# Expert weights in units of one expert's half matrix (16 KB a partition) instead of a quarter of both experts (2 x 8 KB)

## The reference

```python
def expert_block(args):
    tok, e = args
    xb = x_pad[tok]
    gate = jnp.minimum(xb @ w_gate[e] + b_gate[e], SWIGLU_LIMIT)
    up = jnp.clip(xb @ w_up[e] + b_up[e], -SWIGLU_LIMIT, SWIGLU_LIMIT)
    h = gate * jax.nn.sigmoid(SWIGLU_ALPHA * gate) * (up + 1.0)
    return h @ w_down[e] + b_down[e]
```

## Time and profile before

| what | us |
|---|---|
| time, median of 3 runs | 3278.82 (3273.98 to 3283.41) |
| the profiled execution | 3282.47 |
| its span on the core | 3280.6 |
| TensorE busy (matmuls) | 3042.0 |
| vector engine busy | 957.1 |
| scalar engine busy | 476.9 |
| experts: 16 pairs, start of the first gate to the end | 2239.3 to 3280.6 |
| one pair in the middle | 63.60 |

### The profile page before, as it was taken

The page is one execution under the profiler, slowest core; times in us unless marked ns, Lnnn a source line. Parts: engine busy times, 40 slices in busy tenths (PEclk is TensorE's granted clock), DMA queues, the critical chain, the costliest instruction groups (busy, mean ns, idle before and its releaser), DMA issues.

```text
span 3280.6 us, 48447 instructions
## 1 busy us (share of the span) xinstructions
PE 3042.0 (93%) x19571; PEld 2258.1 (69%) x19571; DVE 957.1 (29%) x2650; ACT 476.9 (15%) x628; POOL 102.6 (3%) x194
## 2 busy tenths in 40 slices
PE   8999999999999896886969999958999999999995
PEld 7888888888888785776868888835455445445542
DVE  2342442442343064745630000031112111111214
ACT  2122122122121202011100000000111101111111
POOL 2100100100100000000000000000000000000000
PEclk9999999999999897988989999958999999999998
DMA  6234223224245341422324446526999999999994
GB/s 188 84 98 129 89 94 129 92 91 129 96 100 157 113 129 49 132 73 83 112 75 151 151 153 230 205 65 242 409 408 404 397 408 408 394 409 407 398 404 191
DMA packets 326069, 662.19 MB, mean 202 GB/s; under 512 B 41856, under 2 KB 271360, under 8 KB 275456
## 3 DMA queue, kind: packets, MB, share of 16 engines
q1 hardware_dynamic: 325920, 659.85, 54.7%
HBM read 657.73 MB, written 2.10 MB: 201 GB/s over the span
## 4 chain that ended last, share of the span: by engine, by line
PE 64%; issue 16%; DVE 9%; DVEq 4%; ACT 2%; ACTq 1%; POOL 1%; POOLq 1%; SPq 1%; DMA 0%
PE bank L950 13%; PE bank L831 10%; PE bank L595 9%; PE bank L939 7%; PE bank L981 7%; PE bank L852 3%; PE bank L997 3%; DVE arena L1519 2%; DVE arena L1521 2%; DVEq L1518 2%; PE bank L811 2%; PE bank L655 1%; PE bank L664 1%; PE bank L778 1%; PE bank L668 1%
## 5 line engine op out<-in xcount | busy, mean ns | idle before, releaser
L595 PE MATMUL bank<-arena 128*128 128x256 f32 x4096 | 937.1, 384 | 0.0
L595 PEld LDWEIGHTS bank<-arena 128*128 128x128 f32 x4096 | 770.0, 191 | 114.0 <-issue 7.7
L950 PE MATMUL bank<-arena 128*64 128x512 f32 x2048 | 442.2, 592 | 0.7 <-ACT arena L1219 0.7
L950 PEld LDWEIGHTS bank<-arena 128*64 128x64 f32 x2048 | 146.9, 137 | 292.8 <-issue 291.1
L831 PE MATMUL bank<-arena 128*128 128x256 f32 x1536 | 333.3, 380 | 7.4 <-ACTq L1174 7.4
L831 PEld LDWEIGHTS bank<-arena 128*128 128x128 f32 x1536 | 292.9, 191 | 47.8 <-issue 7.7
L939 PEld LDWEIGHTS bank<-arena 128*128 128x128 f32 x1024 | 224.7, 311 | 15.4 <-issue 12.2
L981 PE MATMUL bank<-arena 128*64 128x512 f32 x1024 | 224.9, 597 | 7.7 <-ACT arena L1229 7.7
L939 PE MATMUL bank<-arena 128*128 128x128 f32 x1024 | 227.8, 384 | 3.1 <-DVEq L1718 3.1
L796 PE MATMUL bank<-arena 128*128 128x256 f32 x1024 | 222.3, 379 | 0.0
L796 PEld LDWEIGHTS bank<-arena 128*128 128x128 f32 x1024 | 194.6, 190 | 26.5
(11 more groups left out here) (289 smaller groups left out, 2318.2 us busy)
## 6 DMA issues: line engine op xcount, KB each, us to landing
arena<-in_w_in_dram SPq DMA_DIRECT2D x72, 2048.0 KB, 8.7
arena<-in_w_gate_dram SPq DMA_DIRECT2D x64, 2048.0 KB, 16.9
arena<-in_w_up_dram SPq DMA_DIRECT2D x64, 2048.0 KB, 13.2
arena<-in_w_down_dram SPq DMA_DIRECT2D x64, 2048.0 KB, 19.2
arena<-in_w_dn_out_dram SPq DMA_DIRECT2D x16, 2048.0 KB, 8.6
arena<-in_w_glu_a_dram SPq DMA_DIRECT2D x8, 2048.0 KB, 8.5
arena<-in_w_glu_b_dram SPq DMA_DIRECT2D x8, 2048.0 KB, 8.4
arena<-in_w_mix_out_dram SPq DMA_DIRECT2D x8, 2048.0 KB, 8.4
```

The lines of the kernel that those rows point to most:

```text
L595: last = mm(ps[bank][:, ct * T:ct * T + T], ring[:, buf, k, ct * P:ct * P + P], rhs[:, k, :], start=k == 0, stop=k == KD - 1)
L950: last = mm(ps[bank][CAP * o:CAP * o + CAP, :], xg[:, 4 * q + k, CAP * o:CAP * o + CAP], w[:, o, k], start=q == 0 and k == 0, stop=q == 3 ...
```

## The change

A unit becomes half of one expert's matrix: 16 KB in a row of memory per partition. Unit numbers in gate, up and down are first + 2 * half + expert. `load_unit` reads one expert with one run per partition; `expand` and `sdown` wait for the two units of a half (one of each expert), then alternate between the experts over all slices of the half (8 slices of the width, or 2 of the hidden width), and give both buffers back with the last matmul that reads each. The number of units, their bytes, the buffers, the count of matmuls and the order in which they are summed stay, as does everything outside these functions.

```diff
--- before.py
+++ after.py
@@ -207,7 +207,7 @@
         wtT = at(TM + 512, T)[0:N_E]
 
 
-        unit = [at(off, 2, 4 * F_E) for off in (OT, OT + 4096, SH + 8192, SH + 12288, SH + 16384, SH + 20480)]
+        unit = [at(off, 8 * F_E) for off in (OT, OT + 4096, SH + 8192, SH + 12288, SH + 16384, SH + 20480)]
         xg = at(0, KD, P)
         sgb = at(2048, F_E)
         ssg = at(2560, F_E)
@@ -382,13 +382,9 @@
 
             def load_unit(j, i):
 
-                kind, quarter = divmod(j, 4)
-                if kind == 2:
-                    src = w_down[ds(2 * i, 2)].rearrange("o (p k) n -> p o k n", k=KF)[:, :, quarter, :]
-                else:
-                    w = w_gate if kind == 0 else w_up
-                    src = (w[ds(2 * i, 2)].rearrange("o (p k) n -> p o (k n)", k=KD)
-                           [:, :, 4 * quarter * F_E:4 * quarter * F_E + 4 * F_E])
+                kind, half, o = j // 4, j % 4 // 2, j % 2
+                w, k = ((w_gate, KD), (w_up, KD), (w_down, KF))[kind]
+                src = w[ds(2 * i + o, 1)].rearrange("o (p k) n -> p (o k n)", k=k)[:, 8 * F_E * half:8 * F_E * half + 8 * F_E]
                 sp.dma_start(unit[j % UNITS], src).then_inc(unit_loaded[j % UNITS], 16)
 
             def reload_unit(j, i):
@@ -941,15 +937,18 @@
                     last.then_inc(xg_done, 1)
 
             def expand(bank, first, i):
-                for q in range(4):
-                    j = first + q
-                    pe.wait_ge(unit_loaded[j % UNITS], 32 * i + 16 * (j // UNITS) + 16)
-                    w = unit[j % UNITS].rearrange("p o (k n) -> p o k n", k=4)
-                    for k in range(4):
+                for h in range(2):
+                    for o in range(2):
+                        j = first + 2 * h + o
+                        pe.wait_ge(unit_loaded[j % UNITS], 32 * i + 16 * (j // UNITS) + 16)
+                    for k in range(8):
                         for o in range(2):
-                            last = mm(ps[bank][CAP * o:CAP * o + CAP, :], xg[:, 4 * q + k, CAP * o:CAP * o + CAP], w[:, o, k],
-                                      start=q == 0 and k == 0, stop=q == 3 and k == 3)
-                    last.then_inc(unit_read[j % UNITS], 1)
+                            j = first + 2 * h + o
+                            last = mm(ps[bank][CAP * o:CAP * o + CAP, :], xg[:, 8 * h + k, CAP * o:CAP * o + CAP],
+                                      unit[j % UNITS][:, k * F_E:k * F_E + F_E],
+                                      start=h == 0 and k == 0, stop=h == 1 and k == 7)
+                            if k == 7:
+                                last.then_inc(unit_read[j % UNITS], 1)
 
             def sgate(i):
                 pe.wait_ge(xg_taken, 4 * i + 4)
@@ -973,16 +972,21 @@
 
             def sdown(i):
                 pe.wait_ge(htr_taken, 2 * i + 2)
-                for k in range(KF):
-                    j = 8 + k
-                    pe.wait_ge(unit_loaded[j % UNITS], 32 * i + 16 * (j // UNITS) + 16)
-                    for n in range(4):
-                        for o in range(2):
-                            last = mm(ps[4 + n][CAP * o:CAP * o + CAP, :], shT[:, k, CAP * o:CAP * o + CAP],
-                                      unit[j % UNITS][:, o, n * 512:n * 512 + 512], start=k == 0, stop=k == KF - 1)
-                        if k == KF - 1 and n < 3:
-                            last.then_inc(sdn_done, 1)
-                    last.then_inc(unit_read[j % UNITS], 1)
+                for h in range(2):
+                    for o in range(2):
+                        j = 8 + 2 * h + o
+                        pe.wait_ge(unit_loaded[j % UNITS], 32 * i + 16 * (j // UNITS) + 16)
+                    for k in range(2):
+                        for n in range(4):
+                            for o in range(2):
+                                j = 8 + 2 * h + o
+                                col = k * D + n * 512
+                                last = mm(ps[4 + n][CAP * o:CAP * o + CAP, :], shT[:, 2 * h + k, CAP * o:CAP * o + CAP],
+                                          unit[j % UNITS][:, col:col + 512], start=h == 0 and k == 0, stop=h == 1 and k == 1)
+                                if k == 1 and n == 3:
+                                    last.then_inc(unit_read[j % UNITS], 1)
+                            if h == 1 and k == 1 and n < 3:
+                                last.then_inc(sdn_done, 1)
 
             def scatter(i, lo, hi, more=True):
                 if lo == 0:
```

## The result

The changed kernel takes 3362.32 us as the median of four runs (3360.02 to 3366.22), against 3277.87 us (3273.98 to 3283.41) of the kernel before: a ratio of 1.0258, 95% interval 1.0238 to 1.0277. That is 84 us more. The profiled execution took 3360.17 us with a span of 3358.3, against 3282.47 and 3280.6. The forecast was 3360 us, in a range of 3338 to 3385.

What follows compares the result with a forecast made beforehand. The prediction took TensorE's own work to bound the expert stage, with transfers following closely. Waits of 66 us plus clock falls of 15 us make 81 us on 3278.8, so 3360 us, in a range of 3338 to 3385.

Steps and rivals of the forecast that it cites:

- The bound, and the lead: Expert stage: TensorE's work is the chain, transfers follow closely; unit 7 of the next pair lands 2.0 us before needed.
- The wait of a pair: In up, TensorE waits 1.5 us at the start and 2.9 in the middle; 4.4 a pair, 15 times, 66 us.
- 0.44 us to the issue: From the release in the middle of down to the issue of the next pair's unit 2: 0.44 us.
- First landing: Unit 2 of the next pair, issued into idle DMA engines, lands 7.1 us after its issue, instead of 7.2.
- Packets of 16 KB: Expert weight loads: fewer, longer runs bring a unit every 4.87 us instead of 4.97.
- The prediction's other figure: Expert weight loads: a fixed cost of about 3 cycles a packet makes larger packets worth 0.03 us a unit.
- The clock: Behind the 2.9 us wait in up, the clock falls in six pairs of ten: 9 x 1.67 = 15 us, bounds 0 and 25.
- The sum: Whole kernel: 66 us of waits plus 15 us of clock falls, 81 us more, giving a median of 3360 us.
- Hidden by a faster queue: Rival: larger packets land unit 7 in time for up, needing 4.15 us a unit; no waits, 3278 us; chance 0.04.
- Slow packets: Rival: 16 KB weight packets are slow like code loads, about 4050 us, or 3391 at a tenth of it; chance 0.08.
- Runs cut into the old 8 KB: Rival: DMA engines cut each weight run into 8 KB; 74 us plus the clock, 3353 to 3378 us; no separate chance.
- Clock held: Rival: the same waits in up, but the clock does not fall; 3342 to 3353 us; chance 0.27.

Runs made afterwards that it cites:

- either part alone: Two runs of the kernel before, old units: given back in pairs at each half's end, 3309.33 us; or awaited two at a time, 3315.78 us.
- the experiment with both edits: Kernel before with its old units and 8 KB runs, both awaited in pairs and given back in pairs: 3370.12 us, ratio 1.0277.
- the early need alone: Kernel before with units given back one by one, but awaited two at a time at each half's start: 3315.78 us, ratio 1.0106.
- down in quarters: Changed kernel, but down's units are again a quarter of both experts, awaited and given back one by one: 3311.41 us, ratio 1.0093.

## Why the prediction was right

**The bound, and the lead.** Right, and shown by experiment. The slack of 2.0 us for unit 7 is used up by either part alone (30 and 37 us) and by both together with a loss over their sum; with half the bytes or one more buffer it is gone.

**The wait of a pair.** Place and order as forecast: two gaps in up, 1.5 and 2.9 us forecast, 1.76 and 2.71 in the pair shown. The size was 4.4 us forecast and 4.92 measured in pairs with the clock held, 15 x 4.92 = 74 us instead of 66. Term by term: 0.44 us to the issue, measured 0.42. First landing 7.1 forecast, 7.3 in the row above and in the mean of pairs 2 to 14. I had let the larger packets shorten it by 0.1 us; with the old packets and the same waits it is 7.4 in the mean, in the kernel before 7.3, so what they take off is within the scatter. Five further units 4.87 us apart, 24.4 us: measured 24.5 (2434.35 to 2458.82). From the landing to the first matmul 0.1 forecast, measured 0.14; and the half behind the gap takes 7.01 us (2458.96 to 2465.97) instead of 6.89, which I had not thought of.

**Packets of 16 KB.** The estimate of 12.5 ns a run, from loads in 1 KB and 8 KB runs, gave 4.87 us a unit against 4.97. It holds nearly: 4.89 us, and 9.80 for two against 9.93 with the old runs in the experiment with both edits; in full stretches 429 to 430 GB/s against 422. The prediction's other figure, 0.03 us a unit, was too low: 0.08 was measured. By the Trainium skill ("DMA: Bandwidth & Descriptors", section "Where 436 GB/s comes from") all transfers together are limited to 435 GB/s. The trace agrees: 432 GB/s over the 24.4 us from 2434.30 to 2458.70, and the waits did not vanish. The 443 of one row above says nothing against it: its share of 1.04 is more than the engines' whole time, so the edges of so short a stretch decide it.

**The clock.** The mechanism was right, the number too high. Nine falls with full effect were forecast, 15 us. In the profiled execution there were six between the first gate and the last down, four of them behind a second gap (2388.74, 2664.28, 3077.24 and 3285.99), where the half then took 8.78 us instead of 7.09: 4 x 1.69 = 7 us. The two behind a first gap (2310.55 and 2930.67) shortened the second to 1.06 and 1.01 us, so that they cost nothing, as forecast. One fall of before, in pair 0's down, did not come, 1.67 us less. This is one execution of four. The others had mean granted clocks of 0.955, 0.952 and 0.953, and the experiment with both edits shows 13 falls at 0.952, so some of them will have had more falls; their times do not follow it (3360.02 us at 0.952).

**The sum.** The stage from the first gate on took 80.7 us more in the profiled execution (from 2236.3 to 3358.3, 1122.0 us, against 2239.3 to 3280.6, 1041.3). The waits are 65.6 us; the 0.23 us that each of 30 stops costs beside its idle time (0.45 of the 4.92 a pair) are 7; the six slow halves are 6 x 1.69 = 10; less 1.67 it is 81. The median lies 84 us higher. The forecast 66 + 15 = 81 has the right sum from one term that was 8 us too small and one that was 8 us too large in this execution; that it fell within 2 us of the median owes something to that.

**The rivals.** Hidden by a faster queue: it would take 505 GB/s, and it was 430. Slow packets: refuted, they are faster than the old. Runs cut into the old 8 KB: refuted, between 2436 and 2438 us 53 packets move 0.87 MB, 16 KB each, and the landings are closer than with the old runs. Clock held (3342 to 3353 us): nearest; its upper end has the waits as they were measured (4.9 us a pair), and what it lacks is above all the falls.

## What to carry over

When buffers are few, look for the moment at which the queue of transfers lies idle, and count from the release that ends it to the last transfer that is needed before the next such moment: that sum against the compute in the same stretch is the lead, whatever the mean shares say. Units that are given back and awaited in pairs take one unit from it at either end, and the second loss is not shared with the first. An arrangement with fewer, longer runs must win more than that by its rate; from 8 to 16 KB the rate rose by 1.6% (a unit every 4.89 us instead of 4.97).

## What was unexpected of the hardware

The length of an idle stretch of TensorE alone does not settle whether the clock falls. In the changed kernel 12 second gaps lasted 2.69 to 2.72 us; behind three of them the clock fell to 0.50, behind nine it stayed at 1.00; with the early need alone gaps of 2.00 and 2.01 us went one way and the other, and in the prediction's rows 1.80 us had held. With gaps between 1.2 and 1.6 us, as with down in quarters, no fall was seen in thirteen pairs. The first transfer into an idle queue lands 7.11 to 7.58 us after its issue in pairs 2 to 14 of the changed kernel, and 7.15 to 7.72 with the old packets and the same waits; the spacing of the five behind it does not scatter (4.88 to 4.90 and 4.97 to 4.98).
